# One sequence-half block on eight cores: first transposes used twice, state products and a state update left out, 32-bit k from scaled activations, last scaling and store in halves

## What is computed

```python
h = modulate(rmsnorm(x, norm1_w[l]), shift1, scale1)      # h * (1 + scale) + shift
p = h @ w_in[l]                                           # q, k, v, g, lr, ...
log_a = log_sigmoid(lr @ w_gate_up[l] + b_gate[l]) / 16
b = cumsum(log_a)                                         # within a chunk
q_dec, k_dec = q * exp(b), k * exp(-b)
scores = where(causal, q_dec @ k_dec.T, 0)
o = scores @ v + q_dec @ s_prev                           # s_prev is 0 for the first chunk
s = exp(b_last) * s_prev + k_end.T @ v                    # state for the next chunk
...
return rmsnorm(x, final_norm_w)
```

## Time and profile before

| | us |
|---|---|
| median of 3 runs | 1268.44 (1268.21 to 1269.2) |
| the profiled execution | 1268.44 |
| its span, first to last instruction, slowest core (0) | 1266.9 |
| spans of cores 0, 2, 4, 6 | 1266.9, 1264.7, 1266.5, 1265.6 |
| spans of cores 1, 3, 5, 7 | 1246.0, 1247.0, 1244.1, 1243.5 |
| core 0: TensorE busy | 1222.1 (96%) |
| core 0: VectorE (DVE), ScalarE (ACT), GpSimd (POOL) busy | 721.5, 432.1, 96.4 |

### The profile page before, as it was taken

The page is one execution under the profiler, slowest core; times in us unless marked ns, Lnnn a source line. Parts: engine busy times, 40 slices in busy tenths (PEclk is TensorE's granted clock), DMA queues, the critical chain, the costliest instruction groups (busy, mean ns, idle before and its releaser), DMA issues.

```text
span 1266.9 us, 20151 instructions; the slowest of 8 cores (1243.5 to 1266.9 us)
## 1 busy us (share of the span) xinstructions
PE 1222.1 (96%) x7050; PEld 660.6 (52%) x7149; DVE 721.5 (57%) x1206; ACT 432.1 (34%) x981; POOL 96.4 (8%) x150
## 2 busy tenths in 40 slices
PE   3899999999999999999999999999999999999996
PEld 2665665555555555555555545555445545544553
DVE  3467876666666543333233476766656656654766
ACT  3487876431111332111111255411121121123553
POOL 3004343200000000000000000000000000000000
PEclk9899999999999999999999999999999999999998
DMA  8930101535346312112222900032120330033222
GB/s 224 243 105 2 51 2 34 117 63 109 63 79 102 70 34 35 34 34 38 44 48 44 311 2 1 12 73 53 29 53 1 67 67 1 1 67 68 85 113 88
DMA packets 16026, 84.42 MB, mean 67 GB/s; under 512 B 2112, under 2 KB 2208, under 8 KB 10288
## 3 DMA queue, kind: packets, MB, share of 16 engines
q0 software_dynamic: 8784, 58.76, 23.4%
q1 hardware_dynamic: 6992, 24.03, 5.1%
q10 hardware_dynamic: 144, 0.26, 0.1%
HBM read 124.40 MB, written 8.91 MB: 105 GB/s over the span
## 4 chain that ended last, share of the span: by engine, by line
PE 92%; DMA 3%; issue 2%; ACT 1%; DVE 1%; POOL 0%; POOLq 0%; DVEq 0%; ACTq 0%
PE psf L489 90%; DMA wsl_a<-w_ada 3%; PE psf L499 2%; ACT hT_a L475 0%; ACT Bt_a L434 0%; DVE Bt_a L482 0%; POOL xb_a L572 0%; DVE h32T_a L444 0%; DVE x_a L456 0%; ACT tmp_a L475 0%; DVE x_a L441 0%; POOL wsl_a L535 0%; ACT tmp_a L434 0%; POOLq L1555 0%; DVE tmp_a L441 0%
## 5 line engine op out<-in xcount | busy, mean ns | idle before, releaser
L489 PE MATMUL psf<-hT_a,wsl_a 128*128 128x384 bf16 (+1 forms) x3461 | 660.1, 346 | 3.7 <-POOL S_bf_a L450 1.1
L489 PEld LDWEIGHTS psf<-hT_a,wsl_a 128*128 128x128 bf16 x3488 | 339.8, 98 | 296.2 <-issue 2.9
L434 ACT ACTIVATE tmp_a<-psf 128x512 f32<-128x512 f32 (+1 forms) x280 | 149.1, 533 | 530.5 <-PE psf L489 518.1
L489 PE MATMUL psf<-wsl_a,aT_a 128*128 128x512 bf16 x1071 | 235.0, 377 | 1.3
L489 PEld LDWEIGHTS psf<-wsl_a,aT_a 128*128 128x128 bf16 x1096 | 107.2, 98 | 126.2
L441 DVE TENSOR_TENSOR tmp_a<-tmp_a,psf 128x384 f32<-128x384 f32 (+1 forms) x80 | 48.7, 608 | 158.6 <-ACT tmp_a L434 158.6
L441 DVE TENSOR_TENSOR aT_a<-tmp_a 128x384 bf16<-128x384 f32 (+1 forms) x128 | 78.6, 617 | 96.1 <-ACT tmp_a L434 94.6
L441 DVE TENSOR_TENSOR x_a<-x_a,tmp_a 128x512 f32<-128x512 f32 x171 | 117.7, 689 | 18.4 <-DVE tmp_a L441 3.5
L441 DVE TENSOR_TENSOR tmp_a<-psf,g2b_a 128x512 f32<-128x512 f32 (+1 forms) x137 | 94.1, 687 | 59.6 <-PE psf L489 58.8
L450 POOL TENSOR_SCALAR S_bf_a<-S_a,dec 128x256 bf16<-128x256 f32 x64 | 58.5, 932 | 126.6 <-DVE S_a L456 126.5
L489 PE MATMUL psf<-cbuT_a,wsl_a 128*128 128x384 bf16 (+1 forms) x313 | 65.0, 346 | 0.4
(11 more groups left out here) (157 smaller groups left out, 902.3 us busy)
## 6 DMA issues: line engine op xcount, KB each, us to landing
wsl_a<-w POOLq DMA_DIRECT2D x16, 1024.0 KB, 9.6
wsl_a<-w_ada POOLq DMA_DIRECT2D x12, 1024.0 KB, 12.5
x_a<-x_cur SPq DMA_DIRECT2D x17, 512.0 KB, 6.4
wsl_a<-w_merge POOLq DMA_DIRECT2D x8, 1024.0 KB, 8.9
out<-x_a SPq DMA_DIRECT2D x16, 512.0 KB, 2.6
wsl_a<-w_conv POOLq DMA_DIRECT2D x8, 768.0 KB, 7.0
xb_a<-x_cur SPq DMA_DIRECT2D x9, 512.0 KB, 4.6
xb_a<-x_cur POOLq DMA_DIRECT2D x8, 512.0 KB, 19.9
```

Source lines behind the costliest of these rows:

```text
L434: P.op("act", lambda e: e.activation(out=out, in_=in_, func=func, **kw), r, w, cost=0.19 + 0.00083 * size(in_) + (0.2 if "accum_out" in kw ...
L489: ins = e.matmul(out=o, lhsT=l, rhs=rh, start=st, stop=sp_)
```

## The change

Even cores: the four transposed banks are copied to SBUF (`xT`), and both `hTs` and `hT` are made from `xT`, so `tr_piece` is not run for the first tile. `xn32` is transposed without waiting for the shift; `special_front` makes `h32s` (scaled only) right after `hTs`, and `special_shift` adds the shift to get `h32T` for q. The 32-bit k product runs on `h32s`, and the shift's share `ks` comes from 32 one-column f32 matmuls of `modT` with `w32k`, added when `kd` is made. The first chunk's product of q with the zero state is left out (4 matmuls). Both kinds of cores: the last chunk's state update is left out (4 matmuls, 4 DVE operations). The last scaling of subtile `NS - 2` and its store are done in two halves, and one multiplication of the last subtile is recorded later.

```diff
@@ special_front, tr and the first tile
-                       xn32.k() + identf.k() + SH, pk, idn=identf.t)
+                       xn32.k() + identf.k(), pk, idn=identf.t)
...
-                        Vts(h32T.t[:, kc, :], p_[:, j * 128:(j + 1) * 128], a1T[:, kc:kc + 1], modT[:, kc:kc + 1],
-                            ALU.mult, ALU.add, pk + ["a1T", ("modT", 0), ("modT", 4)], h32T.k((kc * 128, 128)))
+                        o, i_, rd, wr = h32s.t[:, kc, :], p_[:, j * 128:(j + 1) * 128], pk + ["a1T"], h32s.k((kc * 128, 128))
+                        if half:
+                            Vsmul(o, i_, a1T[:, kc:kc + 1], rd, wr)
+                        else:
+                            A(o, i_, AF.Copy, rd, wr, scale=a1T[:, kc:kc + 1])
+
+            def special_shift():
+                for kc in range(8):
+                    Vsadd(h32T.t[:, kc, :], h32s.t[:, kc, :], modT[:, kc:kc + 1], h32s.k((kc * 128, 128)) + SH,
+                          h32T.k((kc * 128, 128)))
...
+            if first:
+                for kp, (pb, pk) in enumerate(hold):
+                    for j in range(2):
+                        o, i_, wr = xT.t[:, kp * 2 + j, :], pb[:, j * 512:(j + 1) * 512], xT.k(((kp * 2 + j) * 512, 512))
+                        if kp % 2:
+                            Vcopy(o, i_, pk, wr)
+                        else:
+                            A(o, i_, AF.Copy, pk, wr)
             ada(2)
             ada(3)
...
+            if first:
+                special_front()
             k0 = [k_mm(hs, h, 128 if first else 0, T0.w) for h in range(4)]
             ada(0)
             ada(1)
             if first:
+                for h in range(4):
+                    p_, pk = k0[h]
+                    MM([(p_[:, 0:128], w32k.t[:, kc, h * 128:(h + 1) * 128], h32s.t[:, kc, :], kc == 0, kc == 7)
+                        for kc in range(8)], w32k.k() + h32s.k() + pk, pk)
...
             Vcopy(shb[:, 0:5], p_[:, 0:5], pk, ["ce"])
+            if first:
+                p_, pk, _ = bank()
+                MM([(p_[:, h:h + 1], w32k.t[:, kc, h * 128:(h + 1) * 128], modT[:, kc:kc + 1], kc == 0, kc == 7)
+                    for h in range(4) for kc in range(8)], w32k.k() + SH, pk)
+                Vcopy(ks[:, 0:4], p_[:, 0:4], pk, ["ks"])
             run([lr_piece(T0, lr0)])
             run(gate_pieces(T0))
             if first:
-                special_front()
-                run([tr_piece(T0, kc) for kc in range(8)])
+                for kc in range(8):
+                    AV(hT[0].t[:, kc, :], xT.t[:, kc, :], xT.k((kc * 512, 512)) + ["a1T"] + SH, hT[0].k((kc * 512, 512)),
+                       scale=a1T[:, kc:kc + 1], bias=modT[:, kc:kc + 1])
+                special_shift()
@@ k_piece, phaseO, gla_pieces, final_norm
-                    MM([(p_[:, 0:128], w32k.t[:, kc, hs], h32T.t[:, kc, :], kc == 0, kc == 7) for kc in range(8)],
-                       w32k.k() + h32T.k() + pk, pk)
-                    Vtt(kd32.t[:, h, :], p_[:, 0:128], e2[:, 0:128], ALU.mult, pk + e2k, kd32.k((h * 128, 128)))
+                    Vstt(kd32.t[:, h, :], p_[:, 0:128], ks[:, h:h + 1], e2[:, 0:128], ALU.add, ALU.mult, pk + e2k + ["ks"],
+                         kd32.k((h * 128, 128)))
...
+                            if first and g == 0:
+                                mms = [(o_s, l, rh, True, True) for o_s, l, rh, st_, _ in mms if st_]
...
-                out = [phaseA(0), phaseU(0)]
+                out = [phaseA(0)] + ([phaseU(0)] if T.s0 < NS - 1 else [])
...
+                    if s == NS - 2:
+                        for n in range(2):
+                            Vstt(x1v(s, n), x1v(s, n), rstd[:, c:c + 1], fnw.t[:, n * 512:(n + 1) * 512], ALU.mult, ALU.mult,
+                                 x1k(s, n) + [("rstd", c)] + fnw.k((n * 512, 512)) + (x1k(NS - 1, 1) if n else []), x1k(s, n))
+                            store(s, n)
+                        return
```

More of the change, by code:

```diff
@@ L383, in record @@
             hTs = B("hTs", [8, 512], BF16, oA + 16 * KB)
+            xT = B("xT", [8, 512], BF16, oD + 16 * KB)
+            h32s = B("h32s", [8, 128], F32, oA + 24 * KB)
             junk = B("junk", [1024], BF16, oA + 12 * KB)
@@ L882, in record @@
                 wr = hs.k((kc * T0.w, T0.w))
+                if first:
+                    o, pk = xT.t[:, kc, :], xT.k((kc * 512, 512))
                 if kc // 2 % 2:
@@ L990, in f @@
                     p_, pk = k0[h]
-                    hs = slice(h * 128, (h + 1) * 128)
-                    MM([(p_[:, 0:128], w32k.t[:, kc, hs], h32T.t[:, kc, :], kc == 0, kc == 7) for kc in range(8)],
-                       w32k.k() + h32T.k() + pk, pk)
-                    Vtt(kd32.t[:, h, :], p_[:, 0:128], e2[:, 0:128], ALU.mult, pk + e2k, kd32.k((h * 128, 128)))
-                    Vtt(kd.t[:, h, 0:128], p_[:, 0:128], e2[:, 0:128], ALU.mult, pk + e2k, kd.k((h * 512, 128)))
+                    Vstt(kd32.t[:, h, :], p_[:, 0:128], ks[:, h:h + 1], e2[:, 0:128], ALU.add, ALU.mult, pk + e2k + ["ks"],
+                         kd32.k((h * 128, 128)))
+                    Vstt(kd.t[:, h, 0:128], p_[:, 0:128], ks[:, h:h + 1], e2[:, 0:128], ALU.add, ALU.mult, pk + e2k + ["ks"],
+                         kd.k((h * 512, 128)))
                     Vstt(kd.t[:, h, 128:w], p_[:, 128:w], shb[:, h:h + 1], e2[:, 128:w], ALU.add, ALU.mult,
@@ L1170, in gla_pieces @@
                     if s < T.n - 1:
-                        out += [phaseA(s + 1), phaseU(s + 1)]
+                        out += [phaseA(s + 1)] + ([phaseU(s + 1)] if T.s0 + s + 1 < NS - 1 else [])
                     out += [phaseN(s), phaseT(s)]
@@ L1421, in store @@
                     P.op(eng, lambda e: e.dma_start(out=out_d[r, n * 512:(n + 1) * 512], in_=x1v(s, n)), x1k(s, n),
-                         [("out", s, n)], dma=f"h{n}")
+                         [("out", s, n)], dma=f"h{n}" if s == NS - 1 else f"o{n}")
             def final_norm(s):
@@ L1430, in whole @@
                 def whole():
-                    more = x1k(NS - 1, 1) if s == NS - 2 else []
+                    if s == NS - 2:
[4 more added lines that the diff above has]
+                        return
                     Vstt(x1v(s), x1v(s), rstd[:, c:c + 1], fnw.t[:, :], ALU.mult, ALU.mult,
-                         x1k(s) + [("rstd", c)] + fnw.k() + more, x1k(s))
+                         x1k(s) + [("rstd", c)] + fnw.k(), x1k(s))
                     store(s)
@@ L1456, in last_subtile @@
                         Vts(lno[:, 0:1], sso[:, 0:1], 1.0 / D, EPS, ALU.mult, ALU.add, [("sso", 0)], [("lno", 0)])
-                        f_, fk = tmp()
-                        Vtt(f_[:, :], x1v(s, 0), fnw.t[:, 0:512], ALU.mult, x1k(s, 0) + fnw.k((0, 512)), fk)
+                f_, fk = tmp()
+                Vtt(f_[:, :], x1v(s, 0), fnw.t[:, 0:512], ALU.mult, x1k(s, 0) + x1k(s, 1) + fnw.k((0, 512)), fk)
                 flush()
@@ L1525, in record @@
             assert wi[0] == len(plan_), wi
-            P.op("sp", None, [("out", s) for s in range(NS - 1)] + [("out", NS - 1, n) for n in range(2)], [])
+            P.op("sp", None, [("out", s) for s in range(NS - 2)]
+                 + [("out", s, n) for s in (NS - 2, NS - 1) for n in range(2)], [])
         def fill(e, b, n):
```

## The result

Median of 4 runs **1279.04 us** (1279.02 to 1279.46) against 1268.53 for the kernel before in the same job: ratio 1.008, interval 1.0067 to 1.0092. The change costs 10.5 us. Spans of cores 0, 2, 4 and 6: 1277.6, 1277.9, 1275.0 and 1275.2. The forecast of 1269.0 and its range, up to 1272.8, missed this.

What follows compares the result with a forecast made beforehand. TensorE bounds the kernel, and the first q product's start on the even cores decides. +1.9 - 0.45 - 0.45 + 0.3 - 0.7 = +0.6 us gives span 1267.5, time 1269.0 us, range 1264.0 to 1272.8.

Steps and rivals of the forecast that it cites:

- `ks` at 7.0 us: Behind the shift: 32 one-column f32 matmuls as 64 records of 0.109 us, 7.0 us, high bound 7.4.
- the stage at -0.6: First q product to first convolution product: zero-state products -0.45, last update -0.45, three dummies +0.3, together -0.6 us.
- a start behind 65: Sign of being wrong towards slower: first q product starting after 65 us, where 63.5 was forecast.
- a span minus that start over 1205: Sign of being wrong towards slower: span minus first q product's start above 1205 us, where 1204.0 was forecast.
- Ahead of `ada(2)`, up to the shift: Kernel's start: 12 dummies 4.0 us, `ada(3)` +3.1 us, `ada(1)` near 46.6 without DMA wait, shift 3.8 us late.
- From the shift to the gate: Start, behind `ada(1)`: k product, `ks`, split, dummies, gate; first q product at 63.5 against 61.60, +1.9 us.
- Rival 3: Start: clock falls during `ks`, most records take 0.22 us, not 0.11: +5 us there, about 1274 us; chance 0.13.
- Rival 1: Start: one-column f32 products for `ks` take only 1.9 us, q product at 57.7, 1263.2 us; chance 0.15.
- Dummies and gate at half rate: Behind `ks`: 12 dummies take 5.2 us at half clock, gate at 62.5, q product at 63.5.
- Rival 4: Behind the first q product: `kd` and q scalings late on DVE, banks free late, +1 to +3, 1271.3 us; chance 0.12.
- The last update, -0.45: Last chunk's state update left out: four matmuls fewer on TensorE, -0.45 us; its DVE operations lie beside TensorE's work.
- The halves, -0.7: Kernel's end: last scaling and store in halves, 256 KB leave 1.7 us earlier, -0.7 us (0 to -1.0).

Runs made afterwards that it cites:

- e3: Changed kernel without the 12 dummy matmuls ahead of `ada(2)`; 1277.24 us, ratio 1.0062 to the kernel before.
- e1: Changed kernel with the 32 f32 matmuls for `ks` made 128 columns wide, order kept; 1274.98 us, ratio 1.0042 to the kernel before.
- e6: e5 with `ks` from one-column matmuls as in the change; 1273.61 us, ratio 1.0025 to the kernel before.
- e5: Changed kernel repaired: no dummies ahead of `ada(2)`, two k products and wide `ks` behind gate, `hT` later, f32 priced higher, zero-state products kept; 1267.4 us, ratio 0.9982.
- e9: Kernel before with only the four products with the zero state left out; 1269.75 us, ratio 1.0003 to the kernel before.
- e8: Kernel before with only the last state update left out and the last scaling and store in halves; 1268.45 us, ratio 0.9991.
- e4: Kernel before with zero-state products and last update left out, last scaling and store in halves; 1268.01 us, ratio 0.9994.
- e7: e5 without the f32 `ks` product, the shift's share of k taken from the bf16 products; 1265.85 us, ratio 0.9967 to the kernel before.
- e10: e9 without groups of fewer than five dummies; 1271.4 us, ratio 1.0026 to the kernel before.
- e11: e8 without groups of fewer than five dummies; 1268.18 us, ratio 0.999 to the kernel before.
- e12: Changed kernel without groups of fewer than five dummies; 1279.92 us, ratio 1.0084 to the kernel before.

## Why the prediction was wrong, step by step

Two terms of the sum failed: `ks` at 7.0 us, which took 11.24, and the stage at -0.6, which came out at +3.6 to +5.7. Both signs that the prediction gave for being wrong towards slower came: a start behind 65 (68.11) and a span minus that start over 1205 (1209.5).

- **Ahead of `ada(2)`, up to the shift: right.** 12 dummies at the half rate 4.46 us (4.0 taken), `ada(3)` at 28.18 (some 27.95 forecast), `ada(1)` at 46.80 without a wait (46.6), `ks` from 50.48 (50.4). That the start would be late because dummies stand ahead of `ada(2)` and f32 products ahead of `ada(1)` is what happened; e3 gives the dummies' part.
- **From the shift to the gate: the term `ks`, 64 x 0.109 = 7.0 us with a high bound of 7.4, failed. It took 11.24.** The 0.11 us of a record was right at full clock, and its clock was not: the price was taken from records at full clock for a stretch in which the same text expected the clock to fall behind narrow matmuls, in time for the dummies only. Rival 3 said what it would cost if the clock fell during `ks`, and its start, 5 us later, is the one measured. By its own point of decision (before some 25 of the 64 are through) it was close: the fall comes behind 21 to 27. It had 0.13 of the chance, too little. What spoke against it, 32 one-column bf16 matmuls at 0.03 us with the clock at 0.50, says nothing of f32 ones; what spoke for it, an f32 transpose at 0.22 there, was of the same kind. A row that the prediction doesn't use says it plainly, the first 32-bit k product of the kernel before, on core 0 at half clock, 0.23 a record:

```profile
49.63 3.72 PE L489 MATMUL psf<-h32T_a,w32k_a 128*128 128x128 f32 x16
```

Rival 1, with the bf16 pace for f32 (1.9 us), is out: no record of `ks` in the changed kernel took less than 0.11. The failed term is shown by e1 (wide, clock held: 7.39 and a q product at 63.6) and e6 against e5.
- **Dummies and gate at half rate: right** (5.28 for 5.2), 4.2 later with `ks`; 1.46 instead of 1.0 from the gate to the q product. 63.5 + 4.2 + 0.4 is the 68.1 measured.
- **Behind it: -0.45 for the zero-state products and +0.3 for three dummies failed. With the last update the stage was forecast at -0.6 and was +5.2 on core 0.** I priced the instructions that went and came, not the new order. Of the 3.8 on core 4, leaving out the products alone gives 2.5 (e9). The other 1.3 comes with the changed start and is not explained in full: the waits of the stage sum to 6.8 there and to 6.0 in e9. Three at 107 to 110 us (0.72, 0.40, 0.27) are new, two of e9 at 136 to 143 (0.41, 0.64) are gone, and the one for `S_bf` is 0.4 longer, as in e8; no run tries them one by one. e5, which keeps the products and has the changed start repaired, loses 1.7 to 3.2 in the stage, so the products are not the only cause. Cores 0 and 2 lose 1.5 to 2.2 more than 4 and 6. All four wait 1.0 to 1.5 for `w_conv` near 244, and on cores 0 and 2 the clock falls there: the row at 244.01 takes 3.17 us for eight products, against 1.89 at full clock. Rival 4 named stalls of this kind, at +1 to +3; it was too small, and its cause (banks behind `kd`) not the one found.
- **The last update, -0.45: not gained.** The wait for `S_bf` behind it is longer by as much (e8: 0.81 for 0.37; e4 and e9 the same), and the stage is 198.6 to 198.9 with it left out and 198.6 to 198.8 with it. I took four matmuls for time without asking what TensorE would wait for next.
- **The halves, -0.7: the end is 1.9 shorter, and how much of it is theirs is not shown.** From TensorE's end to the span's end it is 12.3 us before, 10.4 in the changed kernel and 10.5 in e8. But it is 10.8 in e9, which has no halves, and 9.7 in e4, which is e9 with the halves and the last update left out. So the halves are worth 1.05 between e9 and e4, while 1.5 come in e9 with no edit at the end. What differs there in e9 is that DVE scales subtile 13 some 0.7 us earlier, and that a trickle of 10 to 20 GB/s behind the stores ends 1.4 us sooner. Whether the order or the execution makes that is open: there is one trace of the kernel before.

Either term alone leads out of the range. Without the clock in `ks` (e1) the time is 1275; and 4.2 us more for `ks` on the forecast of 1269.0, with no loss in the stage, is 1273.2 (an estimate).

## What to carry to other kernels

Price an operation at the clock that its own stretch will have. The one-column f32 matmuls here were busy at 100% in the profile and slow twice: at full clock a record took the same 0.11 us as one 128 columns wide, and the granted clock fell while they ran (in the change and in e6, not in e1 and e5), for what comes behind as well. So look for a way to have such a product in an existing bf16 pass, or leave it out (e7), before making the chain around it cleverer.

Where a list scheduler sets the order, four matmuls fewer can be a new order of everything behind them. Price them from a comparison of the orders and the waits they move, or run that edit alone; and before taking dummies away that stand behind a wait, see what the clock does there.

## What was not expected of the hardware

- Making an f32 product 128 columns wide instead of one made it *faster*: 7.39 us for 11.24 (e1), 1.95 for 3.41 (e5 and e6), all by the granted clock, 1.00 against 0.50, as a record took 0.11 and 0.22 us. At full clock both widths take 0.11.
- Three dummy matmuls of 0.81 us inside a wait cost 0 to 0.6 us, and without them the clock fell behind that wait on some cores of the same program and not on others (e10: core 0 but not core 6). That made e10 slower than e9, by 1.6 us in the medians and 2.9 by the ratios; e11 and e12 show no such loss in the time.
- In the first 20 us the stretches of the profile print a granted clock of 1.00 while matmuls run at half rate: 12 dummies in 4.46 us at 19.14 against 2.75 for 12 at 28.98 in the changed kernel. The trace has no record of the clock before 22.6 us on core 0, and there the dummies change pace: the first nine start 0.43 us apart, the last three 0.22. So the 1.00 ahead of the first record is no measurement.
